# Window and latent attention in the grouped form, short convolution inside the mixer's weight stream, rotation on GpSimd beside the neighbourhood attention

## What is computed

```python
def swa_sink_gqa(x, w_in, sinks, w_o):                # 16 heads of 64, 4 key heads
    qkv = x @ w_in
    q, k, v = rope(q), rope(k), v
    sc = einsum('bnqhgd,bnkhd->bnhgqk', q, k_band) * 64 ** -0.5   # 128 queries, 128 or 256 keys
    m = maximum(max(sc, -1), sink)
    e = exp(sc - m)
    p = e / (sum(e, -1) + exp(sink - m))
    return einsum(p, v_band) @ w_o
def mla(...):                                         # 16 heads, 96 wide, values 64 wide
    p = softmax(causal(einsum(q, k) * 96 ** -0.5)); return (p @ v) @ w_o
def short_conv(b_gate, c_gate, xh, w, bias):          # along the tokens, 256 channels
    return b_gate * dwconv3(c_gate * xh, w, bias)
def gla_prep(q, k, ...):
    q = apply_rope(q, cos, sin); k = apply_rope(k, cos, sin)      # the 512 tokens, not the context
```

## Time and profile before

| | us |
|---|---|
| median of 3 runs | 4760.0 (4756.54 to 4763.3) |
| the profiled execution | 4758.14 |
| its span, first to last instruction | 4756.3 |
| PE busy, share of the span | 3654.1 (77%) |
| DVE busy | 2821.0 (59%) |
| ACT busy | 2143.9 (45%) |
| POOL busy | 647.1 (14%) |

### The profile page before, as it was taken

The page is one execution under the profiler, slowest core; times in us unless marked ns, Lnnn a source line. Parts: engine busy times, 40 slices in busy tenths (PEclk is TensorE's granted clock), DMA queues, the critical chain, the costliest instruction groups (busy, mean ns, idle before and its releaser), DMA issues. The chain is left out here.

```text
span 4756.3 us, 53669 instructions
## 1 busy us (share of the span) xinstructions
PE 3654.1 (77%) x17794; PEld 2957.5 (62%) x17794; DVE 2821.0 (59%) x3774; ACT 2143.9 (45%) x2746; POOL 647.1 (14%) x256
## 2 busy tenths in 40 slices
PE   6975999836866999666975567699897957656987
PEld 5654777635755777445965356588776846345865
DVE  4654999955746999776444544444344555444545
ACT  3433999823526999644433202233232434113433
POOL 0003433400004344300000230000000000310000
PEclk9576999977877999888998777899998978768998
DMA  2014999921017999775211001111121220011222
GB/s 91 1 45 179 419 418 416 402 74 38 1 64 308 417 417 417 298 255 186 60 38 24 1 1 45 37 62 62 58 62 37 73 43 1 1 38 65 97 78 81
DMA packets 158177, 643.31 MB, mean 135 GB/s; under 512 B 43482, under 2 KB 55228, under 8 KB 94396
## 3 DMA queue, kind: packets, MB, share of 16 engines
q1 hardware_dynamic: 135116, 617.42, 34.4%
q0 software_dynamic: 10592, 16.81, 1.0%
q10 hardware_dynamic: 12312, 7.10, 0.7%
HBM read 636.82 MB, written 24.35 MB: 139 GB/s over the span
## 5 line engine op out<-in xcount | busy, mean ns | idle before, releaser
L1413 DVE TENSOR_TENSOR w_low<-w_raw,w_high 128x2048 fp32r<-128x2048 f32 x392 | 881.9, 2283 | 61.6 <-ACT w_high L1477 59.8
L1477 ACT CAST w_high<-w_raw 128x2048 fp32r<-128x2048 f32 x392 | 746.3, 1911 | 78.3 <-DMA w_raw<-in_moe_down_dram 39.2
L485 PE MATMUL banks<-w_high,x_high 128*128 128x512 f32 (+3 forms) x1324 | 518.7, 392 | 145.9 <-DVE w_low L437 134.1
L485 PE MATMUL banks<-w_low,x_high 128*128 128x512 f32 (+3 forms) x1324 | 505.3, 382 | 0.0
L404 ACT CAST w_high<-w_raw 128x512 fp32r<-128x512 f32 (+3 forms) x321 | 190.7, 594 | 695.2 <-PE banks L485 621.1
L485 PE MATMUL banks<-w_high,x_low 128*128 128x512 f32 (+3 forms) x1324 | 503.9, 381 | 0.0
L1317 PE MATMUL banks<-w_high,x_split 128*128 128x512 f32 x1024 | 417.7, 408 | 60.4 <-DVE w_low L1413 54.7
L1317 PE MATMUL banks<-w_low,x_split 128*128 128x512 f32 x1024 | 402.7, 393 | 0.0
L485 PEld LDWEIGHTS banks<-w_high,x_high 128*128 128x128 f32 x1324 | 256.5, 194 | 221.6 <-DVE w_low L437 165.8
L2380 PE MATMUL banks<-x_high,w_high 128*128 128x512 f32 (+1 forms) x1056 | 319.9, 357 | 38.5 <-DVE w_low L2420 38.5
L2380 PE MATMUL banks<-x_high,w_low 128*128 128x512 f32 (+1 forms) x1056 | 323.0, 360 | 0.0
(11 more groups left out here) (375 smaller groups left out, 6999.0 us busy)
## 6 DMA issues: line engine op xcount, KB each, us to landing
w_raw<-in_moe_gate_dram SPq DMA_DIRECT2D x132, 1024.0 KB
w_raw<-in_moe_up_dram SPq DMA_DIRECT2D x132, 1024.0 KB, 10.2
w_raw<-in_moe_down_dram SPq DMA_DIRECT2D x132, 1024.0 KB, 10.9
w_raw<-in_w_ada_dram SPq DMA_DIRECT2D x48, 1024.0 KB, 7.3
w_raw<-in_ffn_w_up_dram SPq DMA_DIRECT2D x44, 1024.0 KB
w_raw<-in_ffn_w_down_dram SPq DMA_DIRECT2D x88, 256.0 KB, 2.7
w_raw<-in_w_cols_dram SPq DMA_DIRECT2D x48, 256.0 KB, 2.6
y<-expert_rows SPq DMA_DIRECT2D x8, 1024.0 KB, 9.8
```

Source lines behind the costliest of these rows:

```text
L485: ins_ = pe.matmul(psum_of(g), st[:, rest % S, a:b], mv[:, rest % S, x:y], start=start and first + second == 0, stop=stop and first == 1)
L1413: dve.tensor_tensor(WS[1][:, v % LOW, :], WR[:, v % RAW, :], WS[0][:, v % HIGH, :].bitcast(F32), ALU.subtract).then_inc(low, 1)
L1477: act.copy(WS[0][:, v % HIGH, :], WR[:, v % RAW, :]).then_inc(high, 1)
```

## The change

- **Window attention.** `a_qT`, `a_k2` and `a_kT` go. A new block `a_split` writes queries and keys as fp32r high and low parts (12 casts on ACT, 12 subtractions on DVE), the two parts of a query head one under the other, those of a key head twice. One transposing block `a_qkT` has 24 groups of four 128x128 transposes, 8 for the keys and 16 for the queries. The scores are two fp32r products with 128 rows. They run through `grouped_attention` with 4 heads to a group, 16 groups, and half of the copies out of PSUM on DVE.
- **Latent attention.** The same operands, in `grouped_attention`, 4 heads to a group.
- **Mixer, both layers.** The setting of `LR` to 1 moves beside the transposes of `modulated` on POOL. The stream's blocks come in the order cols 0, cols 1, w_qk, cols 2, w_v_lr, w_r, w_nav. The convolution runs on DVE inside the stream, one of its steps behind each of the tiles 3 to 6 of cols 2 and of w_v_lr; its last product is two instructions of POOL beside `lrT`. The rotation `rope_g` becomes 24 instructions of POOL beside the neighbourhood attention.

```diff
-    def transpose(self, name, groups):
+    def transpose(self, name, groups, beside=None):
...
+            if beside is not None:
+                @block.gpsimd
+                def _(pool):
+                    beside(pool, aside)
...
-                tiles(dve, tile, leaves_between(leave, False))
+                conv_order = Order(dve, conv_step)
+
+                def convolve(j, stage):
...
+                    gate, o, x, w = SC[:, j, :], SC[:, 2 + j, :], SC[:, 4 + j, :], taps[:, j, :]
...
+                    if stage == 0:
+                        conv_order.done(dve.tensor_tensor(x, x, o, ALU.mult))
+                    elif stage == 1:
+                        conv_order.done(dve.tensor_scalar(o, x, w[:, 1:2], w[:, 3:4], ALU.mult, ALU.add))
...
+                def leaves_and_convolution(c, k):
+                    leaves(c, k)
+                    if convolution is not None and c in (3, 4) and 3 <= k < 7:
+                        convolve(c - 3, k - 3)
+                tiles(dve, tile, leaves_and_convolution)
                 leave_last(leave, False)
...
+                QT = self.sbuf(ctx, "qT", [P, A_HEADS, T], F32R)
+                KT = self.sbuf(ctx, "kT", [P, 2, A_KV, T], F32R)
...
+                    self.split_rows(QKV, QS, KS)
+                    of = lambda x: x.rearrange("p a d -> p (a d)").bitcast(F32)
+                    self.transpose("a_qkT", [([of(KS[:, t, w, h]) for t in range(NT)], KT[:, w, h, :], None, None)
+                                             for w in range(2) for h in range(A_KV)] +
+                                   [([of(QS[:, t, h]) for t in range(NT)], QT[:, h, :], DH ** -0.5, None)
+                                    for h in range(A_HEADS)])
...
-                self.attention("a_attn", units, DH)
...
+                        groups.append(([
+                            ([(QT[:, h, t * P:(t + 1) * P], [KT[:, w, kv, a * P:(t + 1) * P]]) for w in range(2)],
...
+                self.grouped_attention("a_attn", groups, DH, False, 2)
...
+    def split_rows(self, QKV, QS, KS):
...
+                for t in range(NT):
+                    for half in range(2):
+                        act.copy(KS[:, t, 0, :, half, :], k[:, t]).then_inc(k_high, 1)
+                for t in range(NT):
+                    act.copy(QS[:, t, :, 0, :], q[:, t]).then_inc(q_high, 1)
...
-                self.attention("b_attn", units, B_DQ)
+                self.grouped_attention("b_attn", groups, B_V, False, 2)
...
+                def set_ones(pool, done):
+                    pool.memset(LR[:, :, :], 1.0).then_inc(done, 1)
+                    pool.wait_ge(done, 1)
+
+                def finish_convolution(pool, done):
+                    for j in range(2):
+                        pool.tensor_tensor(MX[:, 3 + j, 0:upd * P], SC[:, 2 + j, :], SC[:, j, :],
+                                           ALU.mult).then_inc(done, 1)
+                    pool.wait_ge(done, 2)
...
-                    self.stream(f"u{layer}", MX[:, :, :], KD, blocks)
+                    self.stream(f"u{layer}", MX[:, :, :], KD, cols[0:2] + rows[0:1] + cols[2:] + rows[1:],
+                                (SC, taps, ins["sc_conv"][layer], [(0, T), (T, upd * P)][:1 if last else 2]))
...
-                self.short_convolution(layer, SC, MX, upd)
...
+                    def turn_gla(pool, done):
...
+                            order.done(pool.tensor_tensor(t1, x2, s, ALU.mult))
...
-                        self.rope_halves(f"rope_g{layer}", jobs)
```

More of the change, by code:

```diff
@@ L322, in split, with stream @@
         self.end(sem)
-    def stream(self, name, X, K, blocks):
+    def stream(self, name, X, K, blocks, convolution=None):
         nc, sem = self.nc, self.Sems(self, name)
@@ L393, in tile, with load_taps @@
                     sp.dma_start(W[:, rest, 0:w], src[:, bass.ds(k * w, w)]).then_inc(raw_in[rest], 16)
-                tiles(sp, tile)
+                def load_taps(c, k):
+                    if c == 0 and k == K - 1 and convolution is not None:
+                        sp.dma_start(convolution[1][:, :, :], convolution[2]).then_inc(taps_in, 16)
+                tiles(sp, tile, load_taps)
             @block.scalar
@@ L633, in attention, with grouped_attention @@
         self.end(sem)
-    def grouped_attention(self, name, groups, dv, wide, share, scores_at=None):
+    def grouped_attention(self, name, groups, dv, wide, share, scores_at=None, beside=None):
         nc, sem = self.nc, self.Sems(self, name)
@@ L919, in transpose_rows @@
                                None if bias is None else bias[:, k:k + 1]))
-        self.transpose(name, groups)
+        self.transpose(name, groups, beside)
     def window_layer(self):
@@ L968, in window_layer @@
[L968 to L971 removed]
+                QT = self.sbuf(ctx, "qT", [P, A_HEADS, T], F32R)
+                KT = self.sbuf(ctx, "kT", [P, 2, A_KV, T], F32R)
+                with ExitStack() as c2:
+                    QS = self.sbuf(c2, "q_stacked", [P, NT, A_HEADS, 2, DH], F32R)
+                    KS = self.sbuf(c2, "k_stacked", [P, NT, 2, A_KV, 2, DH], F32R)
+                    self.split_rows(QKV, QS, KS)
[4 more added lines that the diff above has]
+                                    for h in range(A_HEADS)])
@@ L986, in window_layer, with _ @@
+                self.grouped_attention("a_attn", groups, DH, False, 2)
             self.out_projection("a_out", O, ins["a_w_o"])
         self.layer_norm("a_ln", 0, 0)
+    def split_rows(self, QKV, QS, KS):
+        nc, sem = self.nc, self.Sems(self, "a_split")
+        q_high, k_high = sem("q_high"), sem("k_high")
+        q = QKV[:, :, 0:A_HEADS * DH].rearrange("p t (h d) -> p t h d", h=A_HEADS)
+        k = QKV[:, :, A_HEADS * DH:(A_HEADS + A_KV) * DH].rearrange("p t (h d) -> p t h d", h=A_KV)
+        with nc.Block() as block:
+            @block.scalar
+            def _(act):
+                for t in range(NT):
[3 more added lines that the diff above has]
+                    act.copy(QS[:, t, :, 0, :], q[:, t]).then_inc(q_high, 1)
+            @block.vector
+            def _(dve):
+                for t in range(NT):
+                    for half in range(2):
+                        dve.wait_ge(k_high, 2 * t + half + 1)
+                        dve.tensor_tensor(KS[:, t, 1, :, half, :], k[:, t], KS[:, t, 0, :, half, :].bitcast(F32),
+                                          ALU.subtract)
+                for t in range(NT):
+                    dve.wait_ge(q_high, t + 1)
+                    dve.tensor_tensor(QS[:, t, :, 1, :], q[:, t], QS[:, t, :, 0, :].bitcast(F32), ALU.subtract)
+        self.end(sem)
@@ L1784, in modulation, with modulated @@
                                      for layer in range(DEPTH)])
-    def modulated(self, name, layer, which, XT, tiles):
+    def modulated(self, name, layer, which, XT, tiles, beside=None):
         nc, ins = self.nc, self.ins
@@ L1959, in neighbourhood @@
             spare = [MX[:, k, :] for k in (0, 1, 2, 5, 6, 7)]
-            self.grouped_attention(f"na{layer}", groups, DH, True, 3, spare)
+            self.grouped_attention(f"na{layer}", groups, DH, True, 3, spare, beside)
     def gated_linear(self, layer, UG, UR, LR, MX, upd):
```

157 lines of the change are left out of this document (63 added, 94 removed).

## The result

The changed kernel takes 4605.8 us (median of 4 runs, 4604.4 to 4610.2) against 4758.3 (4756.5 to 4763.3): ratio 0.9679, interval 0.9663 to 0.9696. It is 153 us faster; 111 were predicted, and 4605.8 lies under the range of 4611 to 4680. The profiled span is 4602.9 against 4756.3.

What follows compares the result with a forecast made beforehand. No single engine was simply at its peak; barriers end each stage, so gains sum by stage. Terms +10, -52.7, -20, -4.6, -22.3, -19.7, -2 gave -111.3: 4758.1 to 4646.8 profiled, median 4649, range 4611 to 4680.

Steps and rivals of the forecast that it cites:

- Window preparation: Blocks before the window attention: 13.40 us go, `a_split` 9 and `a_qkT` 14.5 come, together 23.5, so +10.
- Window units: Window attention's units: 102 us in place of 154.70 at low clock, so -52.7.
- Which clock? ... I take 0.50: Window attention: clock taken to stay at 0.50, nearer to the old stretch that stayed than to the latent one.
- the clock rises: Rival, window attention: PE without a gap gets full clock, 102 becomes 78, total 4612 to 4622; chance 0.28.
- the 0.65 us wait should go: Window attention: with scores six units ahead, PE's 0.65 us wait per unit for ACT's copy should go.
- Latent attention: Latent attention: 98.5 us from 118.6, so -20; 96 if warm, 109 if the clock falls at the start.
- LR: Mixers: setting `LR` on POOL beside transposes that don't involve POOL saves 4.6 us.
- Convolution: Mixers: blocks of 13.50 and 9.80 us go, last products on POOL beside `lrT` cost +1, so -22.3.
- I take nothing: Mixers' streams: convolution steps on DVE taken to cost nothing, though up to 13 us in both layers if exposed.
- Rotation: Mixers: 10.30 and 10.40 us go, hidden on POOL beside neighbourhood attention, +1 for slowed DVE operations, so -19.7.
- Order of blocks: Mixers' streams: shorter tail against a 14 us PE stall behind cols 2 and a lower clock, -2 in all.
- the added work comes back: Rival: POOL slows attentions' DVE work, convolution steps exposed (+13), latent attention begins cold (+10), total 4684; chance 0.09.

## Why the prediction was wrong

- **Window preparation**, +10: measured +8.8. Right. The transposes had a mean clock of 0.88; the case in which they stay at half clock, 6.5 us more, didn't come. The transposes of the output, in no term of the sum, took 2.3 less.
- **Window units**, -52.7: measured -79.0. The step that failed is "Which clock? ... I take 0.50". The choice compared stretches by waits and by how much a record streams. What it left out was the rows: the old window attention was the one with products of 64, and with 64 rows the new one stays low as well (0.51 over 127.5 us), while with 128 it rises (51.8 us at 1.00). The rival "the clock rises" (0.28, 4612 to 4622) was the case that came, and its 78 met the 75.7. This is 26 us of the miss of 42 (4604.7 against 4646.8 in the profiled executions).
- **Its mechanism**, "the 0.65 us wait should go": wrong. It wasn't a wait for ACT. The size at half clock (1.63 to 1.78 a unit) came out near, 1.60, because the 2.05 it started from was taken from the latent attention, which has no 64-row product, and partly by luck: the scores take 0.57 and not 0.43, the transposes 0.29 and not 0.45, the mixing 0.74. At full clock 1.05 a unit were put down for DVE; it is 1.14 (PE resumes behind its holes at 162.04 and 166.62, four units apart), for the order of DVE's list: with the copy first it is 1.06.
- **Latent attention**, -20: measured -26.2. Right mechanism, mis-sized. 98.5 was 96 plus a hedge for a lost clock; the clock held, and the short units cost less than the 4 us for DVE: 92.4 is 86.4 (16 x 10 x 0.54, given there as 86.6) and 6.0 for all else, which the sum had at 9 and the hedge.
- **LR**, -4.6: -3.7; the transposes beside it took 0.9 more in the two layers. **Convolution**, -22.3: -23.3 and no change in the two `lrT` together; its steps in the stream cost 2 us in the first layer, "I take nothing" was near. **Rotation**, -19.7: -20.7, with 0.3 more in the first attention and 0.4 less in the second. Right.
- **Order of blocks**, -2: the streams gave 3.2 in all; the place of cols 2 alone is worth 8.4, and the convolution's steps take 1.9 and 1.2 back; before, cols 0 and 1 stood late as well, which no run changed by itself, so these don't add up to the 3.2. PE's hole behind cols 2 is 13.5 - 5.3 = 8.2 us, not 14; the clock did fall, to 0.69 there. The mis-sized term is the 14.
- **Untouched stages**, 0: -4 in all; one product took 8 less, which differs between executions, and the others 4 more together.
- The rival that the added work comes back didn't come: with 65 us of work on GpSimd in place of 14 the attentions kept their length, and the steps beside other work cost 4 us where 26 us of blocks went.

The range was too narrow below. It took in the rival's 4612, or its 4622 with the bounds of the latent attention (3) and of the stream (8). But the latent attention came 6.2 under its term, and nothing was left for the differences of untouched stages.

## What to carry to other kernels

Fill the array's rows. Scores with a contraction of 64 cost two changes of rows a unit here and went with 1.2 GHz however closely they were packed; stacking high and low parts, or zeros, under it took 52 us (fp32r, 127.5 to 75.7) and 74 us (float32, 149.8 to 75.9) off the stretch. Full rows weren't enough: with them the ungrouped split form stayed at 0.51 for 113.8 us. An idle time before a weight load that has the same length whichever engine is named is not that engine's: change the form around it and see if it stays. And when two stretches differ in the clock, list all in which their products differ, the rows too, before choosing the one to resemble.

## What the hardware showed that was not expected

- Products of 64 rows: 0.50 over 149.8, 154.7, 200.9 and 385.1 us, with float32 and (127.5 us) fp32r, while the same products with 128 rows ran at 1.00 from the start (75.9 us).
- Going from 128 to 64 rows and back costs 0.59 us a unit at half clock (2.19 against 1.60). Products of 32 rows among fuller ones ran at 1.00 for 13 us all the same.
- More work can be faster: 109.4 us with the float32 product against 113.8 with the cheaper one in the same ring.
- The transposes of `a_qkT` ran at a mean of 0.88, with nothing but transposes on PE.
- GpSimd was busy 65 us beside an attention, and that left DVE's 484 ns, with an input in PSUM, as they were, while a DVE instruction of 128x3 in SBUF went from 170 to 321 ns.
